# Output stage of a hybrid decoder step: order of SyncE's requests, of a GpSimd product and of ScalarE's exponential

## What is computed

```
h    = rmsnorm(x) ; proj = h @ w_in
mix  = [ gated delta rule heads (512) , dilated window attention heads (512) ]
y    = x + mix @ w_out ; out = rmsnorm(y, final_norm_g)
```

## Time and profile before

| | us |
|---|---|
| median of 3 runs | 2167.89 |
| lowest, highest | 2159.40, 2171.67 |
| the profiled execution | 2161.02 |
| its span, first to last instruction | 2159.3 |
| seven rounds of the output loop (1 to 7) | 317.56 |
| mean granted TensorE clock | 0.921 |

### The profile page before, as it was taken

The page is one execution under the profiler, slowest core; times in us unless marked ns, Lnnn a source line. Parts: engine busy times, 40 slices in busy tenths (PEclk is TensorE's granted clock), DMA queues, the critical chain, the costliest instruction groups (busy, mean ns, idle before and its releaser), DMA issues. The chain is left out here.

```text
span 2159.3 us, 30094 instructions
## 1 busy us (share of the span) xinstructions
PE 1884.4 (87%) x9726; PEld 1468.3 (68%) x9726; DVE 757.5 (35%) x1780; ACT 598.7 (28%) x1246; POOL 362.6 (17%) x383
## 2 busy tenths in 40 slices
PE   4799999999999999943749988998899559899997
PEld 2588888888888888712438877887788436555653
DVE  5542225113411341105464444444443332232331
ACT  5421222112211321111105434443445212211221
POOL 4300000000000000012412234223423331211110
PEclk9999999999999999976959989988899559999999
DMA  4222322332234234259847887887767464546470
GB/s 134 65 68 88 98 69 64 93 92 76 62 101 98 62 76 103 81 42 227 241 114 217 270 238 243 263 273 228 244 193 224 130 198 141 167 136 169 138 189 25
DMA packets 264754, 309.80 MB, mean 143 GB/s; under 512 B 70620, under 2 KB 217564, under 8 KB 255148
## 3 DMA queue, kind: packets, MB, share of 16 engines
q1 hardware_dynamic: 253796, 241.13, 42.0%
q10 hardware_dynamic: 10832, 67.01, 8.8%
HBM read 228.51 MB, written 146.44 MB: 174 GB/s over the span
## 5 line engine op out<-in xcount | busy, mean ns | idle before, releaser
L271 PE MATMUL pj<-hT_hi,w_hi 128*128 128x512 f32 (+1 forms) x1056 | 423.6, 401 | 21.1 <-DVE w_lo L477 21.1
L272 PE MATMUL pj<-hT_lo,w_hi 128*128 128x512 f32 (+1 forms) x1056 | 413.3, 391 | 0.0
L273 PE MATMUL pj<-hT_hi,w_lo 128*128 128x512 f32 (+1 forms) x1056 | 413.3, 391 | 0.0
L271 PEld LDWEIGHTS pj<-hT_hi,w_hi 128*128 128x128 f32 (+1 forms) x1056 | 195.8, 185 | 66.9 <-DVE w_lo L477 18.9
L273 PEld LDWEIGHTS pj<-hT_hi,w_lo 128*128 128x128 f32 (+1 forms) x1056 | 195.7, 185 | 46.6 <-issue 1.1
L272 PEld LDWEIGHTS pj<-hT_lo,w_hi 128*128 128x128 f32 (+1 forms) x1056 | 196.1, 186 | 41.7 <-issue 0.9
L1372 PE MATMUL o_ps<-pt,vt 128*65 128x256 f32 (+3 forms) x560 | 148.8, 393 | 3.7 <-DVE ot L1598 3.2
L603 POOL IOTA row_at<- 128x1 int32 x1 | 0.1, 139 | 882.5 <-POOLq L2356 882.5
L1439 ACT ACTIVATE pt<-pt_ps 128x512 f32<-128x512 f32 x144 | 84.6, 587 | 148.8 <-PE pt_ps L1350 147.9
L2120 PE MATMUL y_bank<-wo_hi,mh 128*128 128x512 f32 (+1 forms) x272 | 114.0, 419 | 7.4 <-POOL ml L2105 5.3
L488 DVE SCALAR_TENSOR_TENSOR acc<-raw,conv_wt,acc 128x512 f32<-128x512 f32 x144 | 108.3, 752 | 9.1 <-DVE acc L485 0.3
(11 more groups left out here) (406 smaller groups left out, 3205.3 us busy)
## 6 DMA issues: line engine op xcount, KB each, us to landing
out_dram<-in_cache_k_win_dram ACTq DMA_DIRECT2D x56, 584.0 KB, 7.1
out_dram<-in_cache_v_win_dram ACTq DMA_DIRECT2D x56, 584.0 KB, 6.1
w_raw<-in_w_in_dram SPq DMA_DIRECT2D x35, 512.0 KB, 7.2
kq<-qk_ch SPq DMA_DIRECT2D x64, 256.0 KB, 3.4
qk_ch<-sil SPq DMA_DIRECT2D x32, 256.0 KB, 2.4
z_ch<-xr SPq DMA_DIRECT2D x32, 256.0 KB, 2.5
wqk<-hi SPq DMA_DIRECT2D x32, 256.0 KB, 2.6
wqk<-lo SPq DMA_DIRECT2D x32, 256.0 KB, 2.9
```

What stands on the lines that cost most here:

```text
L271: pe.matmul(out, w_hi[s][:, k, 0:m], hT_hi[:, k, cols], start=(k == 0), stop=False)
L272: pe.matmul(out, w_hi[s][:, k, 0:m], hT_lo[:, k, cols], start=False, stop=False)
L273: mm = pe.matmul(out, w_lo[s][:, k, 0:m], hT_hi[:, k, cols], start=False, stop=(k == KT - 1))
```

## The change

Three orders are rewritten; no instruction of the loop is added, dropped or resized.

- **SP.** A round's requests begin with `lb` and `mx` for both next tiles, 2b+2 and 2b+3 (each behind its wait for `lo`, sums first), then the values of sequence b itself (from round 1 on; those of sequence 0 are asked for ahead of the loop as before), then the keys of b+1, then for each slot the store of y and the x request. Before, tile 2b+3 was asked for between the two stores, and the values of b+1 at the end of the round.
- **POOL.** The product `share(1, b+1)` comes ahead of `root(2b+1)` and not behind it.
- **ACT.** The exponential comes ahead of `high(2b+2)` and not behind it.

```diff
--- before.py
+++ after.py
@@ -2034,12 +2034,18 @@
             load_v(0)
             sp.dma_start(gf[:], D.final_norm_g.unsqueeze(0).to_broadcast([P, D_MODEL])).then_inc(O["const"], 16)
 
-            def store(b, load):
+            def store(b, first, load):
                 if load:
-                    sp.wait_ge(O["lo"], 2 * b + 1)
+                    for u in range(2):
+                        sp.wait_ge(O["lo"], 2 * b + u + 1)
+                        sp.sem_inc(G["seen"], 1)
+                        load_linv(sp, D, env, 2 * b + u + 2, u)
+                        load_mix(sp, D, env, 2 * b + u + 2, u)
+                if not first:
+                    sp.wait_ge(G["mixed"], b)
                     sp.sem_inc(G["seen"], 1)
-                    load_mix(sp, D, env, 2 * b + 2, 0)
-                    load_linv(sp, D, env, 2 * b + 2, 0)
+                    load_v(b)
+                if load:
                     sp.wait_ge(G["far_mm"], NJ * b + NJ)
                     sp.sem_inc(G["seen"], 1)
                     load_rows(sp, D.cache_k, b + 1, kn, kf, k_in)
@@ -2049,19 +2055,11 @@
                     sp.dma_start(D.y[bass.ds(P * (2 * b + u), P), :], yt[:, u, :]).then_inc(out[u], 16)
                     if load:
                         load_x(2 * b + u + 2, u)
-                        if u == 0:
-                            sp.wait_ge(O["lo"], 2 * b + 2)
-                            sp.sem_inc(G["seen"], 1)
-                            load_mix(sp, D, env, 2 * b + 3, 1)
-                            load_linv(sp, D, env, 2 * b + 3, 1)
-                if load:
-                    sp.wait_ge(G["mixed"], b + 1)
-                    sp.sem_inc(G["seen"], 1)
-                    load_v(b + 1)
-
-            with sp.Fori(0, DEC_BATCH - 1) as b:
-                store(b, True)
-            store(DEC_BATCH - 1, False)
+
+            store(0, True, True)
+            with sp.Fori(1, DEC_BATCH - 1) as b:
+                store(b, False, True)
+            store(DEC_BATCH - 1, False, False)
             sp.dma_start(xt[0:NS, 0, :], D.x_sample).then_inc(x_in[0], 16)
             sp.wait_ge(O["done"], NT + 1)
             sp.dma_start(D.y_s, yt[0:NS, 0, :]).then_inc(out[0], 16)
@@ -2096,8 +2094,8 @@
                 share(0, b + 1)
                 low(2 * b + 2, 0)
                 root(2 * b, 0, P)
+                share(1, b + 1)
                 root(2 * b + 1, 1, P)
-                share(1, b + 1)
                 low(2 * b + 3, 1)
             root(NT - 2, 0, P)
             root(NT - 1, 1, P)
@@ -2222,10 +2220,10 @@
             def step(b, more):
                 for j in range(NJ):
                     turned(b, j)
+                act.wait_ge(G["max"], b + 1)
+                act.activation(pr[:], pr[:], ACT.Exp, bias=snmax[:, 0:1], accum_out=slsum[:, 0:1]).then_inc(G["exped"], 1)
                 if more:
                     high(2 * b + 2, 0, b + 1)
-                act.wait_ge(G["max"], b + 1)
-                act.activation(pr[:], pr[:], ACT.Exp, bias=snmax[:, 0:1], accum_out=slsum[:, 0:1]).then_inc(G["exped"], 1)
                 square(2 * b, 0, P)
                 act.wait_ge(G["pT_mm"], b + 1)
                 for w, a, z in ((P, 0, T), (FAR, T, 2 * T), (T, 2 * T, 9)):
```

## The result

| | before | after |
|---|---|---|
| median of 5 runs, us | 2167.89 | 2185.62 |
| lowest, highest | 2155.94, 2171.67 | 2175.18, 2190.28 |
| the profiled execution | 2161.02 | 2182.06 |
| its span | 2159.3 | 2179.6 |
| seven rounds of the output loop | 317.56 | 330.69 |

The changed kernel is slower: the ratio of the times is 1.009, 95% interval 1.0047 to 1.0133. The prediction was 2140.7 us, faster by 1.3%.

A forecast was written before the change was run, and what follows sets the result against it. The prediction took PE as the bound of the last stage; 22.2 us (ACT's order) plus 5.0 us (POOL's order), with SP's order costing 0, made 27.2 us less: 2140.7 us from the 2167.9 us median, range 2127 to 2160 us.

The forecast's parts named there:

- PE is the bound, and the excess over round 7 is what can be had: Output loop, rounds 1 to 7: PE bounds; time above seven rounds of 42.20 us, 22.2 us, is waits and slower clock.
- ACT's order, 22.2 us: Ahead of turn_p: exponential right behind the maximum removes PE's wait for `pr` (14.8 us) and the clock falls; gain 22.2 us.
- what was put down to the clock: Rounds 1 to 5: 7.4 us of the excess is PE's lower clock after the turn_p wait, 1.5 us a fall.
- The 0.13 us by which `low` was to miss the scaling of `pr`: Behind the exponential: `low` starts at 2.17 us, DVE's scaling of `pr` ends at 2.04 us, so they don't overlap.
- POOL's order, 5.0 us, DVE first: Round's head: `scale` starts 0.2 us ahead of `low` and runs through, removing PE's 0.71 us wait at `score`; gain 5.0 us.
- The rival in which POOL gets in first: Round's head: `low` starts first or DVE always pays, -1.4 us in place of +5.0; 2147 us, chance 0.11.
- When the store is asked for and when the values are due: Each round: store of y asked for 4.4 us after the start, values due at `mix` 27.9 us after it.
- When the values land: SP's queue: values land 20.0 to 24.1 us after the store's request, taken as 22; cost 0, at most 4.2 us.
- that "the trickle is partly filled by what stands behind": SP's queue: requests behind partly fill the slow `lb` transfer, the reason for taking 22 us, the middle, for the values' landing.
- The rival in which the values become the bound: Ahead of `mix`: transfers overlap less, values 2.6 us late, 29 us lost against 27 gained; 2170 us, chance 0.06.
- The range: Whole kernel: 2127 to 2160 us, meant for 8 in 10, reaching over POOL first and most of values a little late.
- Its upper bound for the wait: Ahead of `mix`: values at worst 0.6 us late a round, 4.2 us over seven rounds.

## Why the prediction was wrong, point by point

*PE is the bound, and the excess over round 7 is what can be had*: right. With ACT's and POOL's orders alone every round takes 41.46 us, and the sum is 290.21 us where the prediction's steps give 317.56 - 27.2 = 290.4.

*ACT's order, 22.2 us*: right. 21.7 us by itself, including what was put down to the clock: 7.4 us by the prediction, 297.67 - 289.86 = 7.8 us measured. The 0.13 us by which `low` was to miss the scaling of `pr` was enough: that scaling takes 0.68 us in all rounds, with ACT's order alone and in the changed kernel (there with SP's help, since the sums land early).

*POOL's order, 5.0 us, DVE first*: right, 5.6 us. The rival in which POOL gets in first falls. By the rule that the prediction drew from the Trainium skill (SBUF — State Buffer, "SBUF: two separate sides"), whoever starts first keeps the port pair; the trace agrees: 1.28 us for DVE, 3.29 us for the POOL instruction that started 0.24 us later. It agrees roughly, not to the tenth: a full pass behind the release would have taken POOL to 3.42 us, and `scale` in the earlier trace rows ends 0.2 us before a full pass behind 1957.68 would. In the changed kernel `share(1)` lies over `scale(2b)` in every round that has one, 2.27 us in place of 1.28, and only the store waits for it, as the prediction allowed.

*When the store is asked for and when the values are due*: right, 4.4 us and 27.9 us after the round's start.

*When the values land*: wrong, and this step alone turned the sign. The prediction started from the 17.6 us in which y, x, the values and one set (`mx` and a pair of `lb`) are in when the values stand ahead of the set, and added the price of a second set, 2.4 to 6.5 us: 20.0 to 24.1, taken as 22. Measured: 28.3 us on average, 26.2 to 30.0. The experiment with one set ahead parts the miss of 6.3 us.

- The starting point failed, and it is most of the miss. It took those 17.6 us as the same whichever stands in front. With the set in front the same requests take 22.4 to 23.7 us to the end of the values, 5.6 us more on average. Behind the values a set's trickle is hidden: in round 4 of the kernel before the queue moves 163 GB/s or more, microsecond by microsecond from 1967 on, until `lb` is in. In front of them it is not: 41 to 59 GB/s for 4 us in the changed kernel, and 20 to 51 GB/s for 5 us with one set ahead, although `vn` had been asked for there. That "the trickle is partly filled by what stands behind" is what these figures contradict.
- The second set cost 5.1 us more, where 4.4 was taken: within the bounds.

Stage by stage in round 4 of the changed kernel: y and x are in 4.2 us after the store's request, the first set 7.8 us later, the second 9.2 us after that, and the values another 8.1 us: 29.3 us. The row that gave the 6.5 us was a single set that stood last in its burst; it couldn't show what a set does to the requests behind it. The 3.96 us that SP took for a pair of `lb` was noted, but only as time in which SP has nothing else to do; in the changed kernel the request that it puts off is the one that is due. The sums themselves landed when the prediction said, 10.2 to 11.3 us after the request (11 forecast).

*The rival in which the values become the bound* had the mechanism and the point from which it decides (26 us after the request), at a chance of 0.06 and 2170 us. Its price was too low as well: 6.5 us a set, where round 4 has 7.8 and 9.2, and 1.5 us a fall of the clock, where it is 1.8 on average. It also counted seven rounds, and the last asks for no sets: there were six waits. Its loss of 29 us stands against 40.5 us measured.

*The range*, 2127 to 2160 us, left that rival out. Its upper bound for the wait, 0.6 us a round, came from the same sum; the measured wait is 4.9 us on average and up to 6.6 us.

*What a better version is*: the change without SP's part (2142.11 us), or with the values ahead of both sets (2141.45 us). Both are 1.1 to 1.2% faster than the kernel before and 2% faster than the changed one. Their medians come within 1.5 us of the 2140.7 us that the prediction had for the full change: what it forecast is what the kernel does once the values are not behind the sums.

What stays open: why these transfers are slow. The runs show that it is the source, not the size, the pieces or the target. Whether it is the repeated rows or the place of the tensor is not shown; `gf` shows that a repeated row of 4 KB does not do it. A copy of the sums spread over more rows, which would keep the computation and part the two, was not tried.

## What to carry to other kernels

When requests are reordered in one in-order queue, ask for each request that is moved back when it is due and what now stands ahead of it, and price what stands ahead by the slowest row in which such a transfer shows, not by its bytes. The time of a whole burst holds for its order only: a slow transfer behind a large one is partly hidden, the same transfer in front of it is not. A request that holds the issuing engine for microseconds can be a warning that what follows is late, even where the engine itself has nothing to do. And of several parts that remove the same wait, take the one that moves nothing else: here two lines in ACT's order did the work, and the reordered queue could only add a risk.

## What the runs showed of the hardware

A transfer of 128 KB that fills 64 partitions from 4 rows of 512 bytes of one tensor, each read 64 times, landed 9.0 us after its request (median of round 4), and 3.9 us with 256 different rows of another tensor in the same pieces to the same place. While the first pair of them was landing in the changed kernel, the whole queue moved 41 to 59 GB/s. One row of 4 KB read 128 times did not slow the queue so: with it and one `mx` under way it moved 203 GB/s and more.

Behind two such pairs the engine that asks is itself held by its next request, 3.7 to 4.9 us for `vn` in the changed kernel and 5.1 us for the keys in round 4 with the values first, in place of 0.8 to 1.3 us with the different rows. Behind the two `mx` alone the request for `vn` took 1.8 to 2.9 us.

A wait of 5.89 us of PE ended with a granted clock of 0.50 (the lower level), in which the matmuls of `mix` began. In the seven rounds of the kernels in which PE waits at no point for more than 0.74 us (ACT's order alone) the clock was 1.00; in the kernel before and with POOL's order alone, where it waits for `pr`, it fell too.

Of two instructions on DVE and POOL that overlap, the one that started first took its usual time, in both directions: DVE first by 0.24 us, 1.28 us for DVE and 3.29 us for POOL (2.38 alone); POOL first by 0.07 us, 1.29 us for POOL and 2.30 us for DVE (1.28 alone).
